# A fourth set of seven products in the second pair of a down projection, alternating with plain sets

## The reference

```python
FFN_HIDDEN = 5632
h = rms_norm(x, ffn_norm_w[layer], NORM_EPS)
a = jax.nn.silu(jnp.einsum('bsd,df->bsf', h, w_ffn_gate[layer])) * jnp.einsum('bsd,df->bsf', h, w_ffn_up[layer])
x = x + jnp.einsum('bsf,fd->bsd', a, w_ffn_down[layer]).astype(x.dtype)
```

## Time and profile before

| what | us |
|---|---|
| median of 3 runs | 2055.84 (2054.61 to 2057.56) |
| the profiled execution | 2056.46 |
| its span, first to last instruction | 2054.8 |
| TensorE busy | 2046.9 (9530 matmuls) |
| VectorE busy | 1565.0 |
| ScalarE busy | 1164.2 |
| down projection, pair 1, on TensorE | from 1934.3 to 2051.5 |

### The profile page before, as it was taken

One profiled execution on the slowest core, in us unless ns is written; L12 is line 12 of the kernel. 1 busy time (PEld: TensorE's weight loads), 2 busy tenths in 40 slices (PEclk: granted clock), 3 DMA queues, 4 the chain that ended last, 5 costly groups with the idle time before them and its releaser, 6 DMA issues.

```text
span 2054.8 us, 27952 instructions
## 1 busy us (share of the span) xinstructions
PE 2046.9 (100%) x9530; PEld 1688.1 (82%) x9530; DVE 1565.0 (76%) x1860; ACT 1164.2 (57%) x1488; POOL 170.3 (8%) x195
## 2 busy tenths in 40 slices
PE   9999999999999999999999999999999999999999
PEld 8888877778888888888888888888888888887887
DVE  6777866665866777777767887898898889877866
ACT  5444655555556666666655454566666666645543
POOL 1121000000011222222100000000000000000000
PEclk9999999999999999999999999999999999999999
DMA  7656675554566665555565657598888888666574
GB/s 250 198 180 205 194 215 165 173 168 144 183 204 184 184 184 184 184 184 184 165 193 184 211 169 246 174 306 246 258 253 239 251 257 250 198 202 229 180 240 153
DMA packets 220627, 419.80 MB, mean 204 GB/s; under 512 B 16450, under 2 KB 22003, under 8 KB 220291
## 3 DMA queue, kind: packets, MB, share of 16 engines
q1 hardware_dynamic: 212162, 399.48, 61.1%
q0 software_dynamic: 7776, 18.94, 4.3%
q10 hardware_dynamic: 608, 0.34, 0.1%
HBM read 410.25 MB, written 4.26 MB: 202 GB/s over the span
## 4 chain that ended last, share of the span: by engine, by line
PE 97%; DVE 2%; DMA 1%; ACT 0%; issue 0%; SPq 0%; DVEq 0%; ACTq 0%
PE acc L2233 75%; PE side L2320 9%; PE acc L2320 6%; PE side L2249 3%; PE side L2534 1%; DVE w_lo L2025 1%; PE side L2389 1%; DMA w_raw<-in_w_ffn_down 1%; DVE w_raw L1940 0%; DMA x_row<-in_x 0%; PE side L2540 0%; PE acc L2249 0%; PE side L2463 0%; ACT w_hi L1205 0%; PE side L2404 0%
## 5 line engine op out<-in xcount | busy, mean ns | idle before, releaser
L1246 DVE TENSOR_TENSOR w_lo<-w_raw,w_hi 128x1024 fp32r<-128x1024 f32 x332 | 418.9, 1277 | 250.1 <-ACT w_hi L722 248.9
L722 ACT ACTIVATE w_hi<-w_raw 128x1024 fp32r<-128x1024 f32 x332 | 347.9, 1057 | 373.1 <-PE acc L2233 319.4
L2233 PE MATMUL acc<-w_hi,h_hi 128*128 128x512 f32 x1248 | 498.4, 399 | 0.2
L2233 PE MATMUL acc<-w_hi,h_lo 128*128 128x512 f32 x1248 | 487.2, 390 | 0.0
L2233 PE MATMUL acc<-w_lo,h_hi 128*128 128x512 f32 x1248 | 486.0, 389 | 0.0
L2233 PEld LDWEIGHTS acc<-w_hi,h_hi 128*128 128x128 f32 x1248 | 234.4, 188 | 51.0 <-issue 5.6
L2233 PEld LDWEIGHTS acc<-w_hi,h_lo 128*128 128x128 f32 x1248 | 234.2, 188 | 50.4
L2233 PEld LDWEIGHTS acc<-w_lo,h_hi 128*128 128x128 f32 x1248 | 234.7, 188 | 47.9 <-issue 1.9
L1919 DVE TENSOR_TENSOR w_lo<-w_raw,w_hi 128x1024 fp32r<-128x1024 f32 x136 | 165.3, 1222 | 38.0 <-ACT w_hi L1126 35.4
L1042 ACT ACTIVATE w_hi<-w_raw 128x1024 fp32r<-128x1024 f32 x110 | 116.4, 1060 | 116.1 <-PE acc L2233 71.5
L1126 ACT ACTIVATE w_hi<-w_raw 128x1024 fp32r<-128x1024 f32 x136 | 142.9, 1057 | 66.4 <-PE acc L2233 50.9
(11 more groups left out here) (434 smaller groups left out, 3458.6 us busy)
## 6 DMA issues: line engine op xcount, KB each, us to landing
w_raw<-in_w_in SPq DMA_DIRECT2D x320, 512.0 KB, 4.3
w_raw<-in_w_ffn_down SPq DMA_DIRECT2D x88, 512.0 KB, 4.9
w_raw<-in_w_ffn_gate SPq DMA_DIRECT2D x68, 512.0 KB, 4.5
w_raw<-in_w_ffn_up SPq DMA_DIRECT2D x68, 512.0 KB, 5.3
w_raw<-in_w_ssm_proj SPq DMA_DIRECT2D x64, 512.0 KB, 4.4
side_raw<-in_w_ffn_up SPq DMA_DIRECT2D x40, 512.0 KB, 4.6
w_raw<-in_w_attn_proj SPq DMA_DIRECT2D x32, 512.0 KB, 3.7
w_raw<-in_w_out SPq DMA_DIRECT2D x32, 512.0 KB, 4.8
```

Source lines behind the costliest of these rows:

```text
L722: nc.scalar.activation(w_hi[:, r], w_raw[:, n % RING], ACT.Copy).then_inc(hi_ready, 1)
L1246: nc.vector.tensor_tensor(w_lo[:, r], w_raw[:, n % RING], w_hi[:, r].bitcast(F32), ALU.subtract).then_inc(lo_ready, 1)
L2233: done = nc.tensor.matmul(acc[p][:, t], a[:, k0 + kk, cut], w[:, r, kk], start=first and kk == n == 0, stop=last and kk == UK - 1 and n == ...
```

## The change

Pair 1 gets set 8 as a fourth seven, and its order becomes 0, 2, 1, 4, 3, 6, 5, 8, 7, 9, 10: sevens at positions 1, 3, 5 and 7 with one plain set between each two. The table of set 8 is made during set 3 of pair 1, behind its first and third unit; the tables' tensors have room for four. The first combining step goes to the fourth unit of set 7, the plain set behind the last seven. ScalarE's copy of P1's bank in pair 1 waits for the sixth table of the stage in place of the fifth.

```diff
--- before.py
+++ after.py
@@ -95,8 +95,8 @@
 VALUES = [(q, at, n) for q in range(2) for at in range(V_SETS) for n in range(len(PRODUCTS) if V_ORDER[q][at] == V_SEVEN else 4)]
 V_MORE = 2 * (len(PRODUCTS) - 4)
 DOWN_SETS = KF // (2 * UK)
-DOWN_ORDER = ((0, 1, 2, 3, 5, 4, 7, 8, 6, 9, 10), (0, 2, 1, 3, 4, 5, 7, 6, 8, 9, 10))
-DOWN_SEVENS = ((2, 4, 6), (2, 4, 6))
+DOWN_ORDER = ((0, 1, 2, 3, 5, 4, 7, 8, 6, 9, 10), (0, 2, 1, 4, 3, 6, 5, 8, 7, 9, 10))
+DOWN_SEVENS = ((2, 4, 6), (2, 4, 6, 8))
 DOWN_PRODUCTS = ("P1", "P3", "P5", "P2", "P7", "P6", "P4")
 DOWN_SLOT = (0, 2, 0, 3, 1, 2, 3)
 DOWN = [(g, s, n) for g in range(2) for s in DOWN_ORDER[g] for n in range(len(PRODUCTS) if s in DOWN_SEVENS[g] else 4)]
@@ -305,8 +305,8 @@
         s_sum = at("s_sum", 107, [P, 4, UK, P])
         side_raw = [[at(f"side_raw{s}{n}", kb, [P, UK, CW]) for n, kb in enumerate(places)]
                     for s, places in enumerate(((123, 167, 127), (183, 187, 171)))]
-        down_s_hi = at("down_s_hi", 48, [P, 3, 4, UK, P], F32R)
-        down_s_lo = at("down_s_lo", 64, [P, 3, 4, UK, P], F32R)
+        down_s_hi = at("down_s_hi", 48, [P, 4, 4, UK, P], F32R)
+        down_s_lo = at("down_s_lo", 64, [P, 4, 4, UK, P], F32R)
         down_h_sum = at("down_h_sum", 199, [P, 2 * UK, T])
         down_s_sum = at("down_s_sum", 203, [P, 4, UK, P])
         p1_row = at("p1_row", 199, [P, CW])
@@ -1215,12 +1215,12 @@
                 g, s, m = DOWN[n]
                 if n == 6:
                     product_hi(FF // CW - 1)
-                if (g, s, m) in ((0, 1, 1), (0, 5, 1), (0, 8, 1)):
-                    down_sums_hi(((0, 1), (0, 5), (0, 8)).index((g, s)))
+                if (g, s, m) in ((0, 1, 1), (0, 5, 1), (0, 8, 1), (1, 3, 1)):
+                    down_sums_hi(((0, 1), (0, 5), (0, 8), (1, 3)).index((g, s)))
                 if s == DOWN_SEVENS[g][-1] and m == len(PRODUCTS) - 1:
 
                     act.wait_ge(mm_done, unit.now(-LEAD))
-                    act.wait_ge(s_lo_ready, 5)
+                    act.wait_ge(s_lo_ready, 5 + g)
                     nc.scalar.activation(p1_row[:], side[:, 2], ACT.Copy).then_inc(p1_ready, 1)
 
             c = D // CW - 1
@@ -2092,12 +2092,12 @@
                         weights_sum(3, 2, 3)
                 if n == 7:
                     product_lo(FF // CW - 1)
-                for j, (first, last) in enumerate((((0, 1, 0), (0, 1, 2)), ((0, 5, 0), (0, 5, 2)), ((0, 8, 0), (0, 8, 2)))):
+                for j, (first, last) in enumerate((((0, 1, 0), (0, 1, 2)), ((0, 5, 0), (0, 5, 2)), ((0, 8, 0), (0, 8, 2)), ((1, 3, 0), (1, 3, 2)))):
                     if (g, s, m) == first:
                         down_sums(j)
                     if (g, s, m) == last:
                         down_sums_lo(j)
-                if s == (9, 8)[g] and m == 3:
+                if s == (9, 7)[g] and m == 3:
                     combined(g, 0)
                 if s == (10, 9)[g] and m < 3:
                     combined(g, m + 1)
```

## The result

The changed kernel takes 2062.12 us (median of 8 runs, 2059.69 to 2064.4), the kernel before 2056.26 us in the same rounds (2054.61 to 2058.4). The medians are 5.9 us apart. The ratio is 1.0027, 95% interval 1.0016 to 1.0037: some 5.5 us slower. A second set of rounds gave 1.0025 (1.0015 to 1.0036). The forecast was 2059.2, +3.4 us; the measured time lies half a microsecond above the range and beyond the 0.2% that I took for a difference that can be told. Two executions further down, one of half_sums (3276.25 us at a granted clock of 0.584) and the profiled one of swap_three (2259.66 us, 0.851), are left out of the ratios.

The account below looks back on a forecast made before the run. TensorE bounds with a thin lead, transfers second. Stops of 6.5 us against 1.7 now, less 1.4 for the product, give +3.4: 2059.9 for the profiled execution, median 2059.2, range 2056.2 to 2061.6 (own range 2058.4 to 2060.5).

Parts of the forecast that it names:

- The product: Fourth seven of pair 1: six matmuls less on TensorE's path, 9.52 us instead of 10.88, so -1.36 us.
- a fixed chain of 9.28 us: In a seven: ScalarE's copy and VectorE's queue, from slot 2's arrival to issue of slot 1's load after P7's low part.
- the round doesn't close in TensorE's 20.4: Alternating sevens and plain sets: a loop of 22.7 us against 20.4 needed, so 2.3 us lost per round.
- the gaps: TensorE stops before P5 and P7 in sets 4, 6 and 8 of pair 1, released by VectorE's low part; none in set 2.
- the term E to arrival: From slot 1's load issue after P7's low part (E) to the next seven's slot 2 landing, P3's input: 13.4 us.
- slot 2 of the set at position 3 arrives as now, at 1963.23: First alternating round: arrival kept from the earlier profile, now for set 4, whose slot 1 load issues at 1972.51.
- What follows E of the last seven is the same: Tail after the last seven's slot 1 load issue: same plain sets, combining steps and output rows, so the end shifts equally, +3.4 us.
- The table: Made in set 3 between two sevens, delaying slot 2's issue to near E + 9.6: nothing to +1.1 us.
- The stores: Pair 0's rows, queued after the loads of positions 3 and 5, run in the pause: no cost.
- Rival 1: Burst loads arrive as when alone, 3.5 us: loop 20.9 or 20.4, shift -0.2 to -1.1 us; chance 0.07.
- Rival 2: Transfers slower: both rounds at 14.04 us, table's copy +0.7, so +5.4 us; decided beyond mean arrival E + 13.75; chance 0.15.
- each lossy set stops twice: Reading of the kernel before: lossy sevens stop before P5 and P7 for the low part; set 4 lost 1.46 us, set 6 0.22.

Follow-up runs that it names:

- half_sums: Changed kernel with two of the four weight sums in pair 1's sevens on half their columns, output not the reference's: ratio 1.0007 to the kernel before.
- swap_three: Kernel before (three sevens) with the roles of slots 1 and 2 exchanged in the sevens: ratio 1.0001 to the kernel before.
- half_all: Changed kernel with every load of positions 2 to 7 of pair 1 halved, output not the reference's: ratio 0.9997 to the kernel before.
- after: The changed kernel itself, first set of rounds: median 2062.12 us, ratio 1.0027 to the kernel before.
- after_again: The changed kernel once more, no edit: ratio 1.0025 to the kernel before, median 2062.54 us.
- alt_three: Kernel before with its three sevens of pair 1 alternating at positions 1, 3 and 5, no fourth seven or table: ratio 1.0024 to the kernel before.
- table_early: Changed kernel with set 8's table made in set 0 of pair 1 in place of set 3: ratio 1.0040 to the kernel before.
- late_stores: Changed kernel with pair 0's two stores moved behind the loads of positions 9 and 10: ratio 1.0024 to the kernel before.
- spread_four: Changed kernel with pair 1's sevens at positions 1, 4, 7 and 9, combining steps behind the last set: ratio 1.0018 to the kernel before.
- before_again: The kernel before once more, no edit: ratio 1.0000 to the kernel before.
- half_loads: Changed kernel with the loads of plain sets 1, 3 and 5 of pair 1 halved, output not the reference's: ratio 1.0016 to the kernel before.
- half_table_early: Changed kernel with all loads of positions 2 to 7 of pair 1 halved and set 8's table made in set 0: ratio 0.9996 to the kernel before.

## Why the prediction was right and wrong

**Direction and mechanism: right.** The product gives 1.36 us (61.20 against 62.56), the arrival of slot 2 starts a fixed chain of 9.28 us (six rounds of the changed kernel, all at 9.28), the round doesn't close in TensorE's 20.4, and the gaps stand where they were forecast. Both terms were moved: the chain by half_sums with the arrivals unchanged, the arrival by half_all.

**The size: the arrival was taken too low.** The step that failed is the term E to arrival, 13.4 us. The six rounds of the changed kernel have 14.55, 14.07, 13.36, 13.85, 14.10 and 12.69, mean 13.8; all 18 alternating rounds with whole loads and the old product order (after, after_again, alt_three, table_early, late_stores, half_sums, spread_four) have the same mean and reach from 12.35 to 15.17. For three rounds that is 1.1 us more than forecast. My own four readings, 13.92, 13.38, 14.04 and 13.00, have a mean of 13.6 already. I had set the 14.04 aside for its stores, and late_stores shows that the stores don't matter. With 13.6 for the two later rounds the sum would have been +3.8. In the first round, "slot 2 of the set at position 3 arrives as now, at 1963.23" read a moment of one execution as fixed. It was 13.38 after E in that profile, 14.03 in before_again, 14.55 and 13.85 in the changed kernel. This term is about half of the miss; what is known of the rest stands under "The sum now".

**What follows E of the last seven is the same: nearly.** 40.4 and 40.5 us in the kernel before, 41.3 and 40.4 in the changed one. The 41.3 has the gap at 2030.87: the third unit behind the last seven got its raw rows 6.9 us after issue. I had looked for gaps in sevens alone; the plain set behind a late seven has as little lead. The 41.3 is one execution's: late_stores, table_early, half_loads and half_sums have 40.3 to 40.4.

**The table: priced at nothing to +1.1, and 0.4 by the means**, within the scatter, as long as transfers are the limit. The forecast that it puts slot 2's issue at E + 9.6 came true: 9.56 and 9.55 in the changed kernel's two profiles. With quick transfers it costs 22.29 - 20.40 = 1.9 us. It is the next limit, which the prediction didn't name as such.

**The stores** were priced at nothing, and late_stores agrees.

**Rival 1** (loads as when alone) needs half the bytes. Its working has a slip: the 5.8 us is the landing of the fourth unit's rows. The third unit's are issued at E + 1.14, so by the rival's own 3.5 us slot 2 would be issued near E + 6.9 (in half_loads it was, at 6.7, in the rounds without the table), and the loop would close in 20.4, not in 20.9. The Trainium skill's fit (DMA: Bandwidth & Descriptors, Anatomy of one DMA) gives 3.2 us, an estimate, against 3.5 for a lone load here. The page states it for transfers issued from GpSimd, and these are SyncE's; and it is for one transfer, where a burst has four.

**Rival 2** (arrivals of 14.04 twice) had its tipping point at a mean of 13.75, and the measured mean is right on it. Its total, +5.4 us, is what came, but in part by luck: it put E of set 8 at 69.95 us after E of set 2, the forecast at 68.05, and the two profiles have 69.82 and 68.48.

**A reading that was too broad.** The prediction says that each lossy set stops twice. Set 4 does; set 6, with its 0.22 us, has no row.

**The sum now**: rounds +4.3 by two profiles of each kernel, where +3.4 was forecast; after the last E +0.4, which is the one execution with 41.3; the rest of the stage, before E of set 2 where both kernels do the same work, +0.3. That is +5.0 us, against 5.1 to 5.5 by the two ratios and 5.8 to 5.9 by the medians. What isn't settled: the part of one microsecond or so between kernels before this stage and before E of set 2, and why the arrival scatters by 2.8 us among alternating rounds.

## What to carry to other kernels

When an edit makes two heavy steps neighbours, look for the loop that it closes (here: buffer freed, load, copy, sums, buffer freed), add up its parts, and compare with the time that the bound engine needs for one turn; if the loop is longer, the saved work is paid back every turn, however small the averages look. A transfer's time in such a loop must come from bursts of the same density, over several executions, and the spread of its mean belongs in the range. Behind the first limit look for the second: here VectorE's queue needs 22.3 us in the round with the table, less than 1 us below the 23.05 of the transfers' loop (13.77 + 9.28), and 1.9 above TensorE's 20.4.

## What the runs showed of the hardware

Loads of 512 KB, issued 1.14 us apart by one queue, land unevenly. In the changed kernel behind set 4 they are issued at 1974.44, 1975.58, 1976.71 and 1977.85 and land after 5.0, 5.6, 5.8 and 5.9 us, so 1.7, 1.3 and 1.3 us apart, which is a landing rate near 400 GB/s for the last two. Behind sets 2, 6 and 8 the first takes 4.0 to 4.1 us and the second 5.4 to 6.9, so that the second lands 2.5 to 3.9 us behind the first although it was issued 1.14 us later, and the third again 1.3 us behind it. Loads of 256 KB at the same distance (half_table_early, the first four behind sets 2, 4 and 6) took 3.0 to 3.7 us each, with no such step.

Stretches of 1 us of the profile show the DMA engines full in such a burst: behind set 2 of the changed kernel their busy share is 0.93 to 0.97 in each from 1952 to 1958 us, at 231 to 369 GB/s. In half_table_early it is 0.61 to 0.77 in each from 1954 to 1958 us. That fits loads of 512 KB that wait for each other, though no run shows it load by load. I have no cause for the step. It explains the scatter of the arrival only in part: the second load behind E took 5.75 us where the arrival was 14.55, and 6.76 where it was 13.92 (third round of late_stores). Over the 18 rounds slot 2 was issued at E + 8.7 to 10.5 and then took 3.6 to 5.6 us.
